# A fused three-layer kernel on one core: the S5 layer's input product by row blocks, and the cosine products of its states on GpSimd

## The reference

```python
def s5_mixer(h, w_in, log_dt, lam_re, lam_im, b_re, b_im, c_re, c_im, d_skip, w_glu, w_out):
    u = (h @ w_in).astype(f32)                    # 256 x 1024
    ...                                           # a = exp(lam*dt), bb from b: per group and state
    # state recurrence x_t = a * x_(t-1) + bb u_t, complex, 64 groups x 64 states
    # y_t = Re(c x_t), 16 channels a group
    y = y + d_skip.astype(f32) * u
    y = jax.nn.gelu(y).astype(h.dtype)
    y = y * jax.nn.sigmoid(y @ w_glu)
    return y @ w_out
# around it: x = x + rmsnorm(m, mix_post_gain);  h = rmsnorm(x, mix_pre_gain)
```

## Time and profile before

| | us |
|---|---|
| median of 3 runs | 980.24 |
| lowest, highest | 979.63, 980.32 |
| the profiled execution, whole | 980.41 |
| its span | 978.5 |

### The profile page before, as it was taken

The page is one execution under the profiler, slowest core; times in us unless marked ns, Lnnn a source line. Parts: engine busy times, 40 slices in busy tenths (PEclk is TensorE's granted clock), DMA queues, the critical chain, the costliest instruction groups (busy, mean ns, idle before and its releaser), DMA issues.

```text
span 978.5 us, 14303 instructions
## 1 busy us (share of the span) xinstructions
PE 961.0 (98%) x5454; PEld 803.0 (82%) x5454; DVE 581.8 (59%) x637; ACT 507.0 (52%) x727; POOL 309.9 (32%) x333
## 2 busy tenths in 40 slices
PE   8999999999999999999999999999989999999997
PEld 6988878888888888788888888888979888888886
DVE  4899775544554565665764554446686765445444
ACT  5866475444443467445664444435466664444432
POOL 5680458998687326761020000000000010000000
PEclk9999999999999999999999999999999999999999
DMA  9742036666877656545355666558936366557541
GB/s 332 259 157 86 1 117 214 220 222 218 283 225 236 202 195 212 174 130 172 108 193 175 192 192 229 199 174 275 383 140 216 129 189 198 172 178 251 173 171 43
DMA packets 133827, 186.79 MB, mean 191 GB/s; under 512 B 5904, under 2 KB 104720, under 8 KB 133264
## 3 DMA queue, kind: packets, MB, share of 16 engines
q1 hardware_dynamic: 109632, 158.28, 49.7%
q10 hardware_dynamic: 24144, 27.81, 8.2%
HBM read 174.54 MB, written 15.73 MB: 194 GB/s over the span
## 4 chain that ended last, share of the span: by engine, by line
PE 94%; DVE 3%; ACT 2%; issue 1%; POOL 0%; DVEq 0%; POOLq 0%; ACTq 0%
PE ps L519 25%; PE ps L490 17%; PE ps L492 16%; PE ps L491 16%; PE ps L470 2%; PE ps L1064 2%; PE ps L472 2%; PE ps L471 2%; PE ps L848 1%; PE ps L1641 1%; PE ps L1083 1%; PE ps L1074 1%; PE ps L630 1%; PE ps L1169 1%; PE ps L1020 1%
## 5 line engine op out<-in xcount | busy, mean ns | idle before, releaser
L422 DVE TENSOR_TENSOR wlo<-wraw,whi 128x2048 fp32r<-128x2048 f32 x127 | 301.7, 2377 | 291.6 <-ACT whi L416 291.6
L416 ACT ACTIVATE whi<-wraw 128x2048 fp32r<-128x2048 f32 x127 | 243.3, 1916 | 256.9 <-PE ps L492 160.5
L490 PE MATMUL ps<-whi,actH 128*128 128x512 f32 x640 | 257.9, 403 | 1.0 <-ACT qa L2130 0.6
L492 PE MATMUL ps<-whi,actL 128*128 128x512 f32 x640 | 250.2, 391 | 0.0
L491 PE MATMUL ps<-wlo,actH 128*128 128x512 f32 x640 | 249.4, 390 | 0.0
L490 PEld LDWEIGHTS ps<-whi,actH 128*128 128x128 f32 x640 | 120.3, 188 | 27.5 <-issue 2.1
L492 PEld LDWEIGHTS ps<-whi,actL 128*128 128x128 f32 x640 | 120.1, 188 | 26.2
L765 POOL TENSOR_SCALAR ss<-ss 128x1 f32<-128x1 f32 x8 | 1.8, 220 | 436.1 <-ACT sg L735 436.1
L491 PEld LDWEIGHTS ps<-wlo,actH 128*128 128x128 f32 x640 | 120.5, 188 | 22.3
L519 PE MATMUL ps<-whi,gH 128*128 128x512 f32 x248 | 77.8, 393 | 0.0
L519 PE MATMUL ps<-wlo,gH 128*128 128x512 f32 x248 | 76.8, 390 | 0.0
(11 more groups left out here) (454 smaller groups left out, 1573.4 us busy)
## 6 DMA issues: line engine op xcount, KB each, us to landing
wraw<-in_ffn_w_gate SPq DMA_DIRECT2D x44, 512.0 KB, 4.0
wraw<-in_ffn_w_up SPq DMA_DIRECT2D x44, 512.0 KB, 4.9
wraw<-in_ffn_w_down SPq DMA_DIRECT2D x18, 1024.0 KB, 4.9
wraw<-in_fox_w_in SPq DMA_DIRECT2D x16, 1024.0 KB, 5.6
wraw<-in_w_gate SPq DMA_DIRECT2D x22, 512.0 KB, 4.0
wraw<-in_w_up SPq DMA_DIRECT2D x22, 512.0 KB, 5.0
wraw<-in_w_in SPq DMA_DIRECT2D x9, 1024.0 KB, 11.3
wraw<-in_w_down SPq DMA_DIRECT2D x9, 1024.0 KB, 5.1
```

The lines of the kernel that those rows point to most:

```text
L416: act.activation(self.high_of(n0), self.wraw[:, n0 % RAW, :], ACT.Copy).then_inc(self.hi_done, 1)
L422: dve.tensor_tensor(self.low_of(n0), self.wraw[:, n0 % RAW, :], self.high_of(n0).bitcast(F32), ALU.subtract).then_inc(self.lo_done, 1)
L490: pe.matmul(out, xh, wh, start=(ka == 0), stop=False)
L492: last = pe.matmul(out, xl, wh, start=False, stop=(ka == KT - 1))
```

## The change

It has these parts; nothing else of the kernel differs.

- **Entry to S5.** Unit `s` 0 is done by row blocks: `pe_row_turn`, `act_row_turn` and `dve_row_turn` (128 tokens at a time, as the feed-forwards use them already) and the new `mm_tokens`, with the tokens as stationary operand; its 48 products give tokens by features, which ACT copies to `sg` and PE transposes back (`tokens_turned`, 4 transposes) in the middle of unit 1. The 40 fillers go. The order of the squares, norms, adds and row turns on ACT and DVE is rearranged.
- Since the row turns write `actL` early, the low part of the last unit of the second feed-forward's `down` loses its place there (`early_low`, "act") and is written over its raw slot.
- **Unit `s` 3.** Its second half of features goes to bank 0 and DVE may read the first half while it runs (`features_half`).
- **Block 0.** `turn_inputs` does all of `Vc` first, then `Vs`.
- **Rotated states.** The four `X1` products go from DVE to GpSimd, ahead of the column clear; semaphore `rotated` counts both.
- **Outputs.** The gelu's table is loaded before `states_swapped(3)`; the second `turn_outputs` comes after the first tile of the `w_glu` product, whose halves go to banks 0 and 2; ACT's copy `outputs_out(3)` comes after the gelus and high parts of two tiles.
- **First attention.** The `Exp` that loads the table comes after the first two of the copies of `qt`, not before all.
- Two semaphores of the convolution's norm become one (`ln_total`).

```diff
@@ place
-            ("b", R0 + 57344), ("d", self.where["Uall"]), ("qt", self.where["qt1"]),
-            ("act", self.where["actL"]))}
+            ("b", R0 + 57344), ("d", self.where["Uall"]), ("qt", self.where["qt1"]))}
...
-        self.early_low = {f["s"]: early["b"], f["f2.down"] + FT // 2 - 1: early["act"]}
+        self.early_low = {f["s"]: early["b"]}
@@ mm_features, and the new mm_tokens
             out = self.ps[:, bank, f * TOK:(f + 1) * TOK]
+            if second is not None and f == 1:
+                last.then_inc(self.sem("features_half"), 1)
+                out = self.ps[:, second, 0:TOK]
...
+    def mm_tokens(self, pe, st, n0, r, bank):
+        pe.wait_ge(self.lo_done, n0 + 1)
+        out = self.ps[:, bank, r * 256:(r + 1) * 256]
+        for k in range(KT):
+            pe.wait_ge(*self.past(st + "_act_ready", KT * r + k + 1))
+            wh, wl = (t[:, k * 256:(k + 1) * 256] for t in (self.high_of(n0), self.low_of(n0)))
+            xh, xl = self.actH[:, k, r * P:(r + 1) * P], self.actL[:, k, r * P:(r + 1) * P]
+            pe.matmul(out, xh, wh, start=(k == 0), stop=False)
+            pe.matmul(out, xh, wl, start=False, stop=False)
+            last = pe.matmul(out, xl, wh, start=False, stop=(k == KT - 1))
+        if r == RT - 1:
+            last.then_inc(self.used, 1)
@@ dve_postnorm
-        dve.wait_ge(*self.past(st + "_squares", 3))
+        dve.wait_ge(*(self.past(first[:2] + "_second", 1) if st == "pf0" else self.past(st + "_squares", 3)))
         norm(2)
         if turn:
             turn(0, range(4))
         dve.wait_ge(*self.past(st + "_squares", 4))
         norm(3)
         if turn:
-            turn(0, range(4, KT))
+            turn(0, (4, 5) if st == "pf0" else range(4, KT))
         dve.wait_ge(*self.past(st + "_rstd", 2))
         dve.wait_ge(*self.past(st + "_normed", 4))
         for c in range(2):
             add(1, c)
+            if st == "pf0" and c == 0:
+                turn(0, (6, 7))
@@ gpsimd
             for b in range(4):
+                g = slice(16 * b, 16 * b + 16)
                 pool.wait_ge(*m.past("scanned", b + 1))
-                pool.memset(m.X2[:, 16 * b:16 * b + 16, 0:1], 0.0).then_inc(sem("no_state"), 1)
+                pool.tensor_tensor(m.X1[:, g, 1:NCH], m.W[:, b, :].rearrange("p (g c) -> p g c", c=NCH)[:, :, 0:NCH - 1],
+                                   m.CT[:, g, 0:NCH - 1], ALU.mult).then_inc(sem("rotated"), 1)
+                pool.memset(m.X2[:, g, 0:1], 0.0).then_inc(sem("rotated"), 1)
@@ tensor
-            s_first, s_rest, late = m.pe_turn_plain(pe, "s", "pf0_x_ready", (4, 5, 6, 7, 2, 3), 40)
-            m.pe_ffn(pe, "f2", f2_turn, last_units=2, half=lambda: s_first(0), end=lambda: s_first(1))
-            s_rest()
-            for i in range(4):
-                m.mm_features(pe, first["s"] + i, i, ready="s_act_ready" if i == 0 else None,
-                              late=late if i == 0 else None)
+            s_turn = lambda r, part: m.pe_row_turn(pe, "s", "pf0_x_ready", ROWS_HIGH, r, part)
+            m.pe_ffn(pe, "f2", f2_turn, last_units=2, half=lambda: s_turn(0, 0), end=lambda: s_turn(0, 1))
+            m.mm_tokens(pe, "s", first["s"], 0, 0)
+            s_turn(1, 0)
+            s_turn(1, 1)
+            m.mm_tokens(pe, "s", first["s"], 1, 0)
...
+            for i in range(1, 4):
+                if i == 3:
+                    pe.wait_ge(*m.past("ut1", 1))
+                m.mm_features(pe, first["s"] + i, i, middle=tokens_turned if i == 1 else None,
+                              second=0 if i == 3 else None)
@@ turn_inputs
+                parts = ((m.Vc, b, 3 + b),) if b > 0 else ((m.Vc, 0, 1), (m.Vs, 4, 3))
@@ product with w_glu
-            turn_outputs(1)
             for i, k in enumerate(Y_ORDER):
+                if i == 1:
+                    turn_outputs(1)
@@ scalar
+            m.act_heads(act, "a1", m.qt, (0, 4), (4, 5), 0)
             act.activation(rinv[:, 0, 0:1], m.halfpi[:], ACT.Exp)
-            m.act_heads(act, "a1", m.qt, (0, H1), (4, 5), 0)
+            m.act_heads(act, "a1", m.qt, (4, H1), (4, 5), 2)
...
+            m.act_row_turn(act, "s", ROWS_HIGH, 0, (0, 1), MIXPRE + 8)
+            m.act_post_square(act, "pf0", 0, "f2_first", n, 2)
+            m.act_row_turn(act, "s", ROWS_HIGH, 0, (2, 3), MIXPRE + 8)
+            m.act_post_square(act, "pf0", 0, "f2_first", n, 3)
+            m.act_row_turn(act, "s", ROWS_HIGH, 0, range(4, KT), MIXPRE + 8)
...
+            act.activation(m.nmax[:, 0, 0:1], m.halfpi[:], ACT.Gelu_apprx_tanh)
             states_swapped(3)
-            act.activation(m.nmax[:, 0, 0:1], m.halfpi[:], ACT.Gelu_apprx_tanh)
@@ vector, rotate_back
-                dve.wait_ge(*m.past("scanned", b + 1))
-                dve.tensor_tensor(m.X1[:, 16 * b:16 * b + 16, 1:NCH], by_group(m.W[:, b, :])[:, :, 0:NCH - 1],
-                                  m.CT[:, 16 * b:16 * b + 16, 0:NCH - 1], ALU.mult).then_inc(sem("states"), 1)
                 dve.wait_ge(*m.past("w_swapped", 2 * b + 2))
```

More of the change, by code:

```diff
@@ L455, in low_piece, with mm_features @@
                           ALU.subtract).then_inc(done, 1)
-    def mm_features(self, pe, n0, bank, it=0, ready=None, order=range(KT), middle=None, late=None):
-        pe.wait_ge(self.lo_done, n0 + 4 * it + 1)
+    def mm_features(self, pe, n0, bank, order=range(KT), middle=None, second=None):
+        pe.wait_ge(self.lo_done, n0 + 1)
         high, low = self.high_of(n0), self.low_of(n0)
@@ L649, in dve_row_turn @@
                .then_inc(self.sem(st + "_act_ready"), 1)
[L651 to L681, removed]
     def pe_spread(self, pe, st, bank):
@@ L730, in act_post_square @@
             act.wait_ge(*self.past(st + "_scale", 1))
-        act.wait_ge(*(self.past(first, 1), self.past(st + "_normed", 1), self.past(first[:2] + "_second", 1),
-                      (self.used, used))[i])
+        second = self.past("pf0_normed", 3) if st == "pf0" else self.past(first[:2] + "_second", 1)
+        act.wait_ge(*(self.past(first, 1), self.past(st + "_normed", 1), second, (self.used, used))[i])
         if i > 1:
@@ L1660, in _ @@
                 total = pe.matmul(ps[:, 3, 0:TOK], m.ones[:], m.cacc[:, j, :], start=(j == 0), stop=(j == 3))
-            total.then_inc(sem("ln_sum"), 1)
+            total.then_inc(sem("ln_total"), 1)
             m.pe_turn(pe, "ao", (0, 1, 2), n=4)
@@ L1668, in second_sums @@
                                      start=True, stop=True)
-                last.then_inc(sem("ln_second"), 1)
+                last.then_inc(sem("ln_total"), 1)
             def spread_norm():
@@ L1870, in turn_inputs @@
             def turn_inputs(b):
-                pe.wait_ge(*m.past("vc_a", 3 + b if b > 0 else 3))
-                for q in range(4 * b, 4 * b + 4):
-                    cols = slice((q % 4) * P, (q % 4 + 1) * P)
-                    last = pe.transpose(ps[:, b, cols], m.Vc[:, q, :], idn[:])
-                    if b == 0:
-                        last = pe.transpose(ps[:, 4, cols], m.Vs[:, q, :], idn[:])
+                parts = ((m.Vc, b, 3 + b),) if b > 0 else ((m.Vc, 0, 1), (m.Vs, 4, 3))
+                for src, bank, ready in parts:
+                    pe.wait_ge(*m.past("vc_a", ready))
+                    for q in range(4 * b, 4 * b + 4):
+                        last = pe.transpose(ps[:, bank, (q % 4) * P:(q % 4 + 1) * P], src[:, q, :], idn[:])
                 last.then_inc(sem("v_turned"), 1)
@@ L2300, in _, with yg_gelu, yg_high @@
             outputs_out(1)
+            act.activation(m.nmax[:, 0, 0:1], m.halfpi[:], ACT.Gelu_apprx_tanh)
             states_swapped(3)
-            act.activation(m.nmax[:, 0, 0:1], m.halfpi[:], ACT.Gelu_apprx_tanh)
             outputs_out(2)
-            for i, kt in enumerate(Y_ORDER + (None,)):
-                if i == 2:
-                    outputs_out(3)
-                if kt is not None:
-                    act.wait_ge(*m.past("y_sum", i + 1))
-                    act.activation(m.ygT[:, kt, :], m.ygT[:, kt, :], ACT.Gelu_apprx_tanh).then_inc(sem("gelu"), 1)
-                if i > 0:
-                    act.wait_ge(*m.past("gelu", i))
-                    act.activation(m.actH[:, Y_ORDER[i - 1], :], m.ygT[:, Y_ORDER[i - 1], :], ACT.Copy)\
-                       .then_inc(sem("yg_high_ready"), 1)
+            def yg_gelu(i):
+                yg = m.ygT[:, Y_ORDER[i], :]
+                act.wait_ge(*m.past("y_sum", i + 1))
+                act.activation(yg, yg, ACT.Gelu_apprx_tanh).then_inc(sem("gelu"), 1)
+            def yg_high(i):
+                kt = Y_ORDER[i]
+                act.wait_ge(*m.past("gelu", i + 1))
+                act.activation(m.actH[:, kt, :], m.ygT[:, kt, :], ACT.Copy).then_inc(sem("yg_high_ready"), 1)
+            for i in range(2):
+                yg_gelu(i)
+                yg_high(i)
+            outputs_out(3)
+            for i in range(2, KT):
+                yg_gelu(i)
+                if i > 2:
+                    yg_high(i - 1)
```

(3 more changed lines are left out.)

62 lines of the change are left out of this document (36 added, 26 removed), and 2 rows, old and new, of the table KINDS.

## The result

| | before | after |
|---|---|---|
| median, us | 980.12 (6 runs) | 987.25 (6 runs) |
| lowest, highest | 979.33, 980.32 | 986.53, 988.10 |
| ratio | | 1.0075, 95% interval 1.0063 to 1.0087 |
| span of the profiled execution | 978.5 | 985.7 |
| mean granted clock of TensorE | 0.999 | 0.993 |

The change costs 7.1 us. The forecast was 979.1 with a range of 976.3 to 981.1, so the result lies outside, and on the side to which the prediction gave one chance in ten.

What follows compares the result with a forecast made beforehand. PE, with 94% of the chain, was taken as the bound, VectorE from 718 to 738. Heads -1.3, entry -0.9, unit 3 -0.15, rotation with block 0 +1.25 gave -1.1: 979.1 against the median of 980.24, range 976.3 to 981.1.

Steps and rivals of the forecast that it cites:

- The transfers: Loads queued behind the late raw slot: last landing at 721 instead of 713, OTab wanted after 726, so cost nothing.
- An early gain is lost: Rival: DVE keeps the heads' 1.3, or unit `s` 3's load lands behind the tables (1.3); 980.4, chance 0.15.
- a wait of ACT for unit `s` 3's load: Sign in the trace that would prove the rival of unit `s` 3's load landing behind the tables.
- Slower: Rival in the rotation: GpSimd's product on 31 of 32 columns is dear; at 2.3 us each 983.3, chance 0.08.
- Heads, -1.3: First attention: PE's third pair of heads loses its 1.12 us idle; gain 1.3, bounds 0.5 and 1.3.
- Entry -0.9: Entry to S5: unit 0 ends 1.3 earlier, less 0.4 for four more transposes; gain 0.9, bounds 0 and 1.3.
- unit 3 -0.15: Between unit `s` 3 and the `Ur` transposes: of 0.8 us idle on PE only 0.15 is gained.
- block 0 -0.25: Before the first rotation: four `Vc` transposes run in PE's wait for `Vs`; gain 0.25.
- Cosine products: Rotation: four products moved to GpSimd save DVE 1.15 but delay the last scan by 1.35, the fifth `y_sum` by 1.5.
- The hold on DVE: Rotation: DVE and GpSimd take turns at shared memory, making DVE late by 0.3 once and 1.1 twice.
- The full gain (976.4): Rival: GpSimd does not hold DVE at all, last scan 1.15 earlier, total -3.8; chance 0.12.
- turns only in the gaps (977.5): Rival: GpSimd gets its turn only in gaps of DVE, each product costing 0.3, total -2.7; chance 0.15.

Runs made afterwards that it cites:

- small_packets: Changed kernel with the loads of RTab and OTab each cut into four transfers of 1 KB pieces, order of transfers untouched: 993.71 us, ratio 1.0145 to before.
- heads_only: Kernel before with only the first attention's edit, two copies of `qt` ahead of the Exp that loads the table: 978.16 us, ratio 0.9985 to before.
- tables_behind_dve_cosine: Changed kernel with RTab and OTab issued by SP behind the two `glu` units and the four cosine products back on DVE: 977.17 us, ratio 0.9974 to before.
- rtab_behind: Changed kernel with RTab alone issued by SP behind the two `glu` units, OTab left on ACT's queue: 978.18 us, ratio 0.9984 to before.
- tables_behind: Changed kernel with RTab and OTab issued by SP behind the two `glu` units instead of by ACT: 978.39 us, ratio 0.9984 to before.
- otab_behind: Changed kernel with OTab alone issued by SP behind the two `glu` units, RTab left where it was: 978.26 us, ratio 0.9986 to before.
- filler_in_stall: Changed kernel with 30 unused filler products on PE between the transposes of uT and those of `Ur`: 985.09 us, ratio 1.0052 to before.
- round_later: Changed kernel with ACT's rounding and DVE's low part of `glu` unit 1 put behind the `Ur` copies and first block's input work: 981.15 us, ratio 1.0025.

## Why the prediction was wrong

**The transfers (costed at nothing).** This is the step that failed. It put the two `glu` units behind the late slot, and asked only when unit `s` 3 is wanted: "Unit `s` 3's raw data are wanted at 698." That unit landed in 5.0 us. Who waits for the `glu` units was not asked, though the next paragraph names that very instruction, ACT's rounding at 710.86, with the copies of `Ur` behind it. The amount of work for the DMA engines was about right: "whatever lands last does so at 721 instead of 713", and T's first half landed at 719.7 where it had at 714.2. What was wrong is who bears the delay. The prediction gave it to OTab, which has time until 726; but OTab landed at 712.3, only 3.3 later than before, and the second `glu` unit at 714.7, 30 us later than before and 6 behind the time at which ACT wants it. For the two queues move packet for packet, and the weights' are of 1 KB against the tables' 33. Where the bytes were shared evenly, in small_packets, the second unit landed at 695.2, well ahead of 708.4, when ACT wants it. Cost: 6.6 us of standing and 2.6 us of clock by the rows.

**The rival for it.** "An early gain is lost" named the tables, priced at 1.3 with unit `s` 3. It was the right mechanism at the wrong unit, and its sign, a wait of ACT for unit `s` 3's load, did not show. "Slower" was tied to GpSimd's product being dear, from 2.0 us on; its row says 1.6, and that rival fell.

**Heads, -1.3.** Measured -1.46 (heads_only).

**Entry -0.9, unit 3 -0.15, block 0 -0.25.** Measured together 0.99 with the outputs, forecast 1.3. By the rows of tables_behind_dve_cosine, set against heads_only: the last product of unit 3 starts 1.9 earlier, less 0.9 by which this execution is ahead from its start (the third pair at 60.60 against 61.50), so 1.0 for the entry; from there to the transposes of `Ur` 0.1 more; from those to the first rotation 5.0 instead of 5.4, so 0.4 for block 0. The sizes hold; of the 1.5 that the rows show, 1.0 reaches the end.

**Cosine products.** Forecast 1.35 at the last scan and 1.5 at the fifth `y_sum`; the scan came 1.22 later relative to the first rotation (15.40 against 14.18). The price in the median is 1.22 with everything else of the change in place, and 0.57 in the kernel before; why less arrives there stays open. The hold on DVE is as read from the earlier trace rows: a turn behind GpSimd costs 1.07 (1.75 - 0.68), twice, and 0.26 once. The full gain (976.4) and turns only in the gaps (977.5) are refuted.

**The sum.** Without the transfers' term it was right: forecast 1.1 under before, measured 1.2 to 1.5 with the stall removed in three ways. Some of that is errors that cancel: the heads gave 0.2 more than forecast, entry and what follows 0.3 less, and the cosine products cost 0.3 less at `y_sum`. One term at zero was worth more than all the others.

## What to carry to other kernels

When an edit delays a buffer's release, follow every transfer that is queued behind it to its first reader, and then to what stands behind that reader in its in-order queue: the reader itself may have time, the next instruction not. Count what is in flight in that stretch, on the other queues first, and not only its bytes but the size of its packets. Issue the small pieces that are wanted soon before the large ones that are wanted late. A stand of TensorE of several us is to be priced with the slow products behind it, here 7 us with some 2 more.

## What the hardware showed that I had not expected

- Two transfers of 1 MB on SP's queue took 20 and 33 us beside tables of 4 MB on ACT's, which themselves took 16.4 and 19.1, against 12.9 and 15.9 before. From 690 to 716 the engines moved 386 to 433 GB/s. The two queues moved packet for packet, 1 KB against 33. With table pieces of 1 KB the two took 7.7 and 13.6.
- An issue is not always short. Four issues of RTab in pieces of 1 KB held ACT for 11.9 us. In rtab_behind a single issue behind the `glu` units held SP for 3.5:

```profile
L1476 SPq DMA_DIRECT2D RTab<-R_dram x1: 3473/3473/3473, 682.0 to 682.0; - x1
```

The transfer itself is not the reason: the same issue took 0.34 us on ACT's queue, and that of OTab 0.34 on SP's in tables_behind, where RTab was ahead of it, but 4.0 in otab_behind, where the `glu` units' small packets still were. So what is outstanding on the queue counts; which measure of it holds the issuing engine was not separated.
- Two of the kernels with late loads vary more from run to run: filler_in_stall from 983.89 to 990.56 and round_later from 980.42 to 986.01, against 986.53 to 988.10 in the change and 977.48 to 978.68 in tables_behind. The one trace of each shows the first `glu` unit later than in the change (27.3 and 23.5 us against 19.8). Whether that is what makes their long runs is not shown.
